# Attention over the paged cache: the first item's keys turned earlier, page loads held back, a new order of the steps around the window riders

## The chip, the cores and the metric

One core of one Trainium2 chip runs the whole program. The metric is the device time of one execution in microseconds, the median of several. Below, PE is TensorE (PEld its weight loads), DVE is VectorE, ACT is ScalarE, POOL is GpSimd and SP is SyncE, which here only issues transfers.

## The reference, cut to what matters

One decoder layer is computed for a prompt of 2048 positions and for 8 samples of 8 new positions each. The change lies where the samples' latent attention (`mla_sample`) begins: every sample attends to 8192 past positions that lie in pages of a cache, with 8 heads that share one latent key of width 256 and one rotary key of width 32.

```python
ckv_past = cache_ckv[l, page_table].reshape(Bd, past, KV_LORA)
kr_past = cache_krope[l, page_table].reshape(Bd, past, QK_ROPE)
...
s_past = jnp.einsum('bthc,bkc->bhtk', q_lat, ckv_past) + jnp.einsum('bthr,bkr->bhtk', q_rope, krope_past)
...
p, _ = masked_softmax_stats(jnp.concatenate([s_past, s_new], axis=-1) * MLA_SCALE, mask)
...
return (jnp.einsum('bhtk,bkc->bthc', p[..., :P], ckv_past)
        + jnp.einsum('bhtk,bkc->bthc', p[..., P:], ckv_new))
```

Beside it each sample has a dilated window attention over its last 2048 keys (`dilated_sample`, three patterns) and a cross-attention into 256 memory tokens. All these outputs are gated, projected and added to the residual.

## The kernel before, in words

The program is a chain of stages, each a block in which every engine runs its own list of instructions: input projection, the prompt's windows, latent projections, `prompt_latent_attention`, then a block with `sample_attention` and the output projection. Engines wait for each other only by semaphores, and within an engine the order is that of the code. A barrier (L3077) stands between the blocks.

**The prompt's attention** works on 32 units (`NU`), each two heads by 256 queries. An order `STEPS` made once and walked by all engines mixes scores, turns of probabilities (`turn`), values and the turning back of outputs (`back`). DVE copies half of every turned block (`keep_turned`, L1867) and does the last division (`finish`, L1877). The last two units are short (two and one pair of key blocks). POOL ends this stage with indirect loads (L1693 to L1699) of the first three pages of the cache (`EARLY` = 3), each of 1024 positions, and of their rotary keys.

**The samples' attention** takes the pages two by two: an item n is the pages 2n and 2n+1 of one sample, and there are 32 items (`NPAIR`), four to a sample. Item by item:

- DVE turns the keys (`turn_keys(l, k)`, L2455 for the two halves of a page, L2457 for the rotary keys); a page's pieces raise `k_turned` by 3. Before the loop it turns pages 0 and 1; in the loop it turns the pages of item n+1 while PE works on item n, except that for n = 0 the maximum of item 0 comes first.
- PE computes the scores in two parts, `score(n, 0, 4)` and `score(n, 4, CB + 1)`. By the trace's count the first is 64 matmuls and the second 80, the last 16 of them rotary (all L2179). Between and behind them stand parts of the values of the item before, `value(n - 1, lo, hi)` (L2214), positions 0 to 2 (12 matmuls) and 3 to 7 (20 matmuls). The end of positions 3 and 7 raises `pv_done`.
- DVE takes the maximum (`maxima`, L2463, L2464), ACT the exponentials (L2382), PE turns the probabilities (`turn_probs`, L2201, 16 matmuls), ACT copies them (L2375), DVE adds up (`accumulate`).

**Riders.** The window and memory attention of the 8 samples ride on items: `RIDES` = {3: 0, 6: 1, 9: 2, 13: 3, 16: 4, 19: 5, 23: 6, 26: 7}. At the end of such an item PE turns the window's keys (`turn_rows`, L2230), does the item's values, and scores the first 1024 keys (`score_rows(s, 0)`, L2256). The next item, the rider item (`rider_before(n)` gives its sample s), does the rest: window probabilities of both parts are turned (`turn_rows_probs`, L2268, L2270) and copied by ACT (`keep_rows_probs`, L2395), the second part is scored (`score_rows(s, 1)`, L2243 to L2246), and both parts' values are made (`value_rows`, L2286 and L2278 to L2280). DVE takes their maxima (`maxima_of_rows`, L2471) and copies the results (L2493).

**Loads.** POOL loads pages by `load_page(l)`: an indirect load of rotary keys (L2113) and one of the latent rows (L2118), 8 slots ahead (`AHEAD`). Pages 3 to 9 are issued without a wait; the later ones wait for `k_turned` and for `pv_done` of the page that was in the slot. SP loads the window of sample s (`load_window`, nine issues for keys, nine for values, and the memory's), the first one when `pv_done` reaches 3.

Of the kernel before, what the change touches and what calls it, by code (L numbers as in the profile page):

```python
# [17 lines left out]
P = 128  # L18
# [512 lines left out]
class Host:  # L531
# [7 lines left out]
    def __init__(self, b, zero, ident):  # L539
# [3 lines left out]
        self.pages_loaded, self.pages_kr_loaded = ([b.sem(f"{n}_loaded{l}") for l in range(self.EARLY)] for n in ("page", "page_kr"))  # L543
        self.k_raw = self.buf[:, 0:SEQ]
# [869 lines left out]
def prompt_latent_attention(nc, io, prompt, sample, host, owner):  # L1414
# [98 lines left out]
    with ExitStack() as stack:  # L1513
# [7 lines left out]
        pages_ahead = b.sb("pages_ahead", [P, Host.EARLY - 1, SEQ])  # L1521
        q_parts = b.sb("q_parts", [P, QBUF, 4, CW], F32R)
# [317 lines left out]
        def vector(dve):  # L1840
# [39 lines left out]

            dve.wait_ge(masks, 1)

            for what, a, p in STEPS:
# [6 lines left out]
                elif what == "turn":  # L1890
                    keep_turned(a, p)
                elif what == "back":
                    finish(a)

        return FirstUnit(load_first, load_third, cast_first, cast_third, split_first, split_third), pages_ahead, Programs(sync, gpsimd, tensor, scalar, vector)


# [26 lines left out]
def sample_attention(nc, io, sample, late, host, pages_ahead, stack, memory, owner):  # L1924


    GK = 8 * PAGE
# [100 lines left out]
    def sync(sp, output):  # L2028
# [74 lines left out]
    def gpsimd(pool):  # L2103
# [20 lines left out]
        pool.wait_ge(k_turned, 3 * EARLY)  # L2124
# [28 lines left out]

    def lanes_of(k, c, r):
# [6 lines left out]
    def tensor(pe, output):  # L2161
        def score(n, lo, hi):
# [3 lines left out]
            for k in range(lo, hi):  # L2166
                for h in range(2):
                    for g in range(4):
                        lanes = slice(UNIT * g, UNIT * g + UNIT)
                        out = scores[h * Q:(h + 1) * Q, g, 0:2 * P]  # L2170
                        if k < CB:
                            lhs = q_quad[lanes, s % 2, k, :]
                            rhs = turned[n % 2][lanes, :, h * HALF:(h + 1) * HALF, k * UNIT:(k + 1) * UNIT]
                            out = out.rearrange("q (i m t) -> q i m t", i=2, t=UNIT)
                        else:
                            lhs = q_rot[lanes, s, :]
                            rhs = krT[lanes, n % 2, :, h * P:(h + 1) * P]
# [5 lines left out]
        def wait_for_keys(n, s):  # L2183
# [7 lines left out]
            pe.wait_ge(k_turned, 6 * n + 6)  # L2191
# [114 lines left out]
        for n in range(NPAIR):  # L2306
# [23 lines left out]
            if s is not None:  # L2330
                value_rows(n, s, 1)
# [31 lines left out]
    def scalar(act, output):  # L2363
# [39 lines left out]
        for n in range(NPAIR):  # L2403
            s = rider_before(n)
            if s is not None:
                exponentials_of_rows(s, 0)
                keep_rows_probs(s, 0)
                exponentials_of_rows(s, 1)
            if n == LEFT + 1:
# [6 lines left out]
            if s is not None:  # L2416
# [816 lines left out]
```

## Time and profile before

| | |
|---|---|
| median of 3 runs | 1922.42 us (1918.53 to 1926.72) |
| the profiled execution | 1921.31 us, its span 1919.7 us |
| PE busy | 1795.3 us, 94% of the span |
| DVE, ACT, POOL busy | 1081.9, 810.2, 416.0 us |
| first score of item 0 starts | 1071.7 us from the span's start |
| exponentials of item 0, of item 31 start | 1092.5 us, 1515.9 us |

The span is what the profiler saw of one execution. Times of single instructions below are microseconds from the span's start. Matmuls overlap, so that PE's busy share says little about its pace; the idle time before an instruction and what ended it say more.

### The profile page before, as it was taken

The numbers are of one execution on the slowest core, as the hardware profiler recorded it, in microseconds if no ns is written. First come the engines' busy times: TensorE is split into PE (matmuls) and PEld (weight loads), VectorE is DVE, ScalarE is ACT, GpSimd is POOL, SyncE is SP. The second block draws the span as 40 slices with busy tenths as digits, with TensorE's granted clock in tenths as the row PEclk, the third lists the DMA queues.
The fourth block names the chain that finished last, engine by engine and source line by source line (L and its number), as shares of the span: only waits on it lengthen the run. The fifth ranks groups of instructions, "written<-read, shape, count | busy, mean of one in ns | idle before, by whom it ended". The sixth has DMA issues, their size and how long they took to land. (4 is left out here: it accounts for less than half of the span.)

```text
span 1919.7 us, 46575 instructions
## 1 busy us (share of the span) xinstructions
PE 1795.3 (94%) x18256; PEld 1370.1 (71%) x18256; DVE 1081.9 (56%) x2808; ACT 810.2 (42%) x1778; POOL 416.0 (22%) x567
## 2 busy tenths in 40 slices
PE   7999999999999899999999588988888889999998
PEld 6988988767787666776776355555555678888886
DVE  5443433787745677677766465666656853333343
ACT  5332322887723455565555132222222543333332
POOL 0101101274021230232012322232322311211110
PEclk9999999999999999999999699999999999999999
DMA  8746554733476410121102587888985574444441
GB/s 297 178 101 138 118 114 109 238 114 121 126 197 198 147 41 18 48 75 33 27 18 97 197 226 224 247 247 248 249 244 203 173 197 124 139 126 126 145 135 65
DMA packets 301372, 281.58 MB, mean 147 GB/s; under 512 B 146008, under 2 KB 262568, under 8 KB 292264
## 3 DMA queue, kind: packets, MB, share of 16 engines
q1 hardware_dynamic: 282840, 186.60, 38.1%
q0 software_dynamic: 18352, 92.44, 13.0%
q8 instruction: 130, 2.13, 0.5%
q14 instruction: 50, 0.41, 0.1%
HBM read 215.09 MB, written 55.48 MB: 141 GB/s over the span
## 5 line engine op out<-in xcount | busy, mean ns | idle before, releaser
L104 PE MATMUL proj_acc<-proj_w_hi,proj_x_hi 128*128 128x512 f32 (+2 forms) x512 | 182.4, 356 | 10.8 <-DVE proj_x_lo L362 8.7
L105 PE MATMUL proj_acc<-proj_w_lo,proj_x_hi 128*128 128x512 f32 (+2 forms) x512 | 181.9, 355 | 0.0
L106 PE MATMUL proj_acc<-proj_w_hi,proj_x_lo 128*128 128x512 f32 (+2 forms) x512 | 181.7, 355 | 0.0
L1851 DVE CUSTOM_DVE_ANT_0 mla_probs<-mla_scores,keep_in_rms 128x512 f32<-128x512 f32 x192 | 124.8, 688 | 59.4 <-PE mla_scores L1725 59.1
L1801 ACT ACTIVATE mla_probs<-mla_probs,mla_bias 128x256 f32<-128x256 f32 (+15 forms) x128 | 153.1, 1197 | 8.1 <-DVE mla_bias L1855 7.0
L1725 PE MATMUL mla_scores<-prompt_kr_parts,mla_q_parts 64*128 64x512 f32 (+3 forms) x640 | 135.3, 367 | 0.0
L2382 ACT ACTIVATE dec_probs<-dec_scores,sample_nb 128x1024 f32<-128x1024 f32 x32 | 35.7, 1114 | 207.5 <-DVE sample_nb L2464 176.9
L104 PEld LDWEIGHTS proj_acc<-proj_w_hi,proj_x_hi 128*128 128x128 f32 x512 | 97.4, 190 | 22.2 <-issue 8.7
L105 PEld LDWEIGHTS proj_acc<-proj_w_lo,proj_x_hi 128*128 128x128 f32 x512 | 97.5, 190 | 10.6
L106 PEld LDWEIGHTS proj_acc<-proj_w_hi,proj_x_lo 128*128 128x128 f32 x512 | 97.3, 190 | 10.4
L2179 PE MATMUL dec_scores<-late_turned,sample_q_lat 32*64 32x256 f32 x2048 | 85.2, 398 | 20.8 <-issue 12.0
L883 ACT ACTIVATE win_probs<-win_probs,win_rec 128x256 f32<-128x256 f32 (+1 forms) x192 | 86.8, 456 | 18.4 <-DVE win_rec L919 18.1
L1750 PEld LDWEIGHTS mla_turned<-host_ident,mla_probs 64*128 64x128 f32 x2180 | 80.5, 140 | 15.7 <-ACT mla_probs L1801 8.7
L1725 PE MATMUL mla_scores<-mla_even_k_hi,mla_q_parts 64*128 64x512 f32 (+3 forms) x320 | 80.2, 407 | 9.6 <-DVE mla_lowest L1851 7.8
L1750 PE MATMUL mla_turned<-host_ident,mla_probs 64*128 64x64 f32 x2180 | 84.7, 224 | 4.6 <-ACT mla_probs L1801 4.5
L106 PE MATMUL fin_gate<-fin_wg_hi,fin_x_lo 128*128 128x512 f32 x224 | 87.2, 389 | 0.0
L104 PE MATMUL fin_gate<-fin_wg_hi,fin_x_hi 128*128 128x512 f32 x224 | 87.2, 389 | 0.0
L105 PE MATMUL fin_gate<-fin_wg_lo,fin_x_hi 128*128 128x512 f32 x224 | 87.1, 389 | 0.0
L2179 PEld LDWEIGHTS dec_scores<-late_turned,sample_q_lat 32*64 32x64 f32 x2048 | 50.9, 135 | 49.0 <-issue 42.6
L2179 PE MATMUL dec_scores<-dec_keysT,sample_q_lat 32*64 32x256 f32 x2048 | 77.6, 394 | 7.4 <-issue 4.0
L1851 DVE CUSTOM_DVE_ANT_0 mla_probs<-mla_scores,mla_mask 128x256 f32<-128x256 f32 (+3 forms) x128 | 57.7, 488 | 46.5 <-PE mla_scores L1725 45.8
L1664 POOL CAST mla_q_parts<-host_buf 128x256 fp32r<-128x256 f32 x31 | 12.8, 414 | 314.3 <-DMA host_buf<-mla_qr 162.8
(462 smaller groups left out, 4490.3 us busy)
## 6 DMA issues: line engine op xcount, KB each, us to landing
featT<-proj_blocks SPq DMA_DIRECT2D x68, 180.0 KB, 4.9
win_v_tile<-wv_out SPq DMA_DIRECT2D x75, 128.0 KB
memory_x_raw<-in_xT SPq DMA_DIRECT2D x17, 512.0 KB, 5.4
proj_rows<-in_x SPq DMA_DIRECT2D x17, 512.0 KB, 3.8
late_ckv<-in_xT SPq DMA_DIRECT2D x17, 512.0 KB, 6.7
late_ckv<-in_x SPq DMA_DIRECT2D x17, 512.0 KB, 3.9
y_out<-host_buf POOLq DMA_DIRECT2D x16, 512.0 KB, 6.5
late_ckv<-late_ckv SPq DMA_DIRECT2D x248, 32.0 KB, 1.8
```

Of the source, the lines that this page charges most:

```text
L104: pe.matmul(out, lh, rh, start=start, stop=False)
L105: pe.matmul(out, lh, rl, start=False, stop=False)
L106: return pe.matmul(out, ll, rh, start=False, stop=stop)
L883: act.activation(pr, pr, ACT.Exp, bias=low[:, h:h + 1], scale=-1.0, accum_out=total[:, h:h + 1]).then_inc(exp_done, 1)
L1664: pool.tensor_copy(qn_hi[:, v, :], qn_raw[:, u % 2, :]).then_inc(q_high, 1)
L1725: mm = pe.matmul(scores[:, at % 3, 0:n], lhs[rows, :], rhs[rows, :], start=a == 0, stop=a == len(parts) - 1)
L1750: mm = pe.transpose(turned[:, r % 2, lane, (kb * 2 * QB + w) * 64:(kb * 2 * QB + w + 1) * 64], probs[rows, u % 2, w, src * P:(src + 1) * P ...
L1801: act.activation(row, row, ACT.Exp, bias=bias[:, at:at + 1], scale=-1.0, accum_out=total[:, at:at + 1]).then_inc(exp_done, 1)
L1851: dve.tensor_tensor_reduce(probs[:, u % 2, w, c * CH:c * CH + wide], scores[:, n % 3, 0:wide], add, -MLA_SCALE, -LOWEST, ALU.add, ALU.min, ...
L2179: mm = pe.matmul(out, lhs, rhs, start=k == 0, stop=k == CB)
L2382: act.activation(probs[:].rearrange("p j (r k) -> p r j k", r=4), scores[:, :, 0:2 * P].rearrange("p r (j k) -> p r j k", k=UNIT), ACT.Exp ...
```

## The change

There are three parts.

1. The keys of item 0 (pages 0 and 1) are turned by DVE at the end of the prompt's attention, in six pieces, two behind each of the three last copies of turned blocks (`turn_first_keys`). They go to a part of the prompt's `probs` buffer that the last unit doesn't use, and have a semaphore of their own, `first_keys`. `k_turned` so counts 6 fewer everywhere.
2. In the samples' block, `load_page(6)` and all that is behind it on POOL wait for the scores of item 0, and so do SP's first four loads.
3. Order. In rider items PE scores the second part of the window first, then turns the first part's probabilities, does three quarters of the remaining latent scores, turns the second part's probabilities, ends the scores and does both value groups ahead of `turn_probs`; ACT copies the second part's probabilities ahead of the item's exponentials; DVE takes the second maximum ahead of the second page's first half. In the other items, values 0 and 1 instead of 0 to 2 stand between the two parts of the scores and values 2 to 7 behind.

```diff
@@ prompt_latent_attention
+        first_keys = probs[:, 1, :, :].rearrange("p (i h) t -> p i h t", i=2)
+        KEYS_AT, KR_AT = SEQ // 2, SEQ // 2 - host.KR
...
+            def turn_first_keys(k):
+                l, half = divmod(k, 2)
+                if k == 0:
+                    dve.wait_ge(ring_done, last_turn(NU - 5) + 1)
+                    dve.wait_ge(ring_done, last_turn(NU - 3) + 1)
+                if k < 4:
+                    src = pages_ahead[:, 0, :] if l else host.page
+                    dve.wait_ge(host.pages_loaded[l], 16)
+                    dve.transpose(first_keys[:, l, half, KEYS_AT:], src[:, half * KEYS_AT:(half + 1) * KEYS_AT]).then_inc(host.first_keys, 1)
+                else:
+                    dve.wait_ge(host.pages_kr_loaded[half], 16)
+                    dve.transpose(first_keys[:, half, 0, KR_AT:KEYS_AT], host.pages_kr[half]).then_inc(host.first_keys, 1)
...
                 elif what == "turn":
                     keep_turned(a, p)
+                    if a >= NU - 2 and pieces < 6:
+                        for k in range(pieces, pieces + 2):
+                            turn_first_keys(k)
+                        pieces += 2
@@ sample_attention, sync
+        sp.wait_ge(scores_done, 1)
         for dst, f in ((qbT, FB_QB), (kbT, FB_KB), (qcT, FB_QC)):
@@ gpsimd
             if l >= AHEAD + EARLY:
-                pool.wait_ge(k_turned, 3 * (l - AHEAD) + 3)
+                pool.wait_ge(k_turned, 3 * (l - AHEAD) - 3)
+            if l == AHEAD - 2:
+                pool.wait_ge(scores_done, 1)
...
-        pool.wait_ge(k_turned, 3 * EARLY)
+        pool.wait_ge(k_turned, 3 * EARLY - 6)
@@ tensor
+    def keys_at(n, h):
+        if n == 0:
+            return first_keys[:, :, h, SEQ // 2:].rearrange("p i (m c) -> p i m c", c=KVL)
+        return turned[n % 2][:, :, h * HALF:(h + 1) * HALF, :]
...
-            pe.wait_ge(k_turned, 6 * n + 6)
+            if n:
+                pe.wait_ge(k_turned, 6 * n)
+            else:
+                pe.wait_ge(host.first_keys, 6)
...
             if s is not None:
+                score_rows(s, 1)
                 turn_rows_probs(n, s, 0)
-                score_rows(s, 1)
+                score(n, 4, 7)
+                turn_rows_probs(n, s, 1)
+                score(n, 7, CB + 1)
+                value_rows(n, s, 0)
+                value_rows(n, s, 1)
             elif n:
-                value(n - 1, 0, 3)
-            score(n, 4, CB + 1)
-            if s is not None:
-                value_rows(n, s, 0)
-                turn_rows_probs(n, s, 1)
-            elif n:
-                value(n - 1, 3, M)
+                value(n - 1, 0, 2)
+                score(n, 4, CB + 1)
+            else:
+                score(n, 4, CB + 1)
+            if s is None and n:
+                value(n - 1, 2, M)
...
             turn_probs(n)
-            if s is not None:
-                value_rows(n, s, 1)
@@ scalar
                 exponentials_of_rows(s, 1)
+                keep_rows_probs(s, 1)
...
             exponentials(n)
-            if s is not None:
-                keep_rows_probs(s, 1)
@@ vector
-        for l in range(2):
-            for k in range(3):
-                turn_keys(l, k)
...
-                turn_keys(2 * n + 3, 0)
                 if s is not None:
                     maxima_of_rows(s, 1)
+                turn_keys(2 * n + 3, 0)
```

## Rows read from the trace of the kernel before

**Rows 1.** Windows around the start of the sample attention, all engines

```profile
1066.00:1072.00 6.00, 0.32 (x8) 0.35 (x16) 5.28 (x6) 0.00 (x0) 3.98 (x5) 0.50 0.59 165
...
1072.00:1091.00 19.00, 14.33 (x144) 7.40 (x131) 0.02 (x1) 0.00 (x0) 10.85 (x12) 0.59 0.98 394
...
1091.00:1098.00 7.00, 1.33 (x24) 1.18 (x32) 6.96 (x9) 2.41 (x4) 2.02 (x3) 0.50 0.07 18
```

**Rows 2.** Timeline, item 0: start us, us, engine, line, what, idle before

```profile
1066.26 2.37 DVE L2455 STREAM_TRANSPOSE late_turned<-host_buf 128x1024 f32<-128x1024 f32 x2 [2.43 <-PEq L3077]
...
1066.81 0.96 POOL L2113 DMA_INDIRECT dec_kr<-in_cache_kr,sample_rows_of  x1 [23.28 <-POOLq L3077]
...
1071.65 2.45 PEld L2179 LDWEIGHTS dec_scores<-late_turned,sample_q_lat 32*64 32x64 f32 x50 [8.58 <-issue]
...
1077.88 0.21 PEld L2179 LDWEIGHTS dec_scores<-late_turned,sample_q_lat 32*64 32x64 f32 x4 [1.22 <-issue]
...
1083.19 0.95 POOL L2118 DMA_INDIRECT late_ckv<-in_cache_ckv,sample_rows_of  x1 [0.30 <-issue]
...
1086.39 2.44 PEld L2179 LDWEIGHTS dec_scores<-late_turned,sample_q_lat 32*64 32x64 f32 x50 [1.23 <-issue]
...
1090.98 1.23 DVE L2463 TENSOR_REDUCE dec_gmax<-dec_scores 128x1 f32<-128x1024 f32 x1 [19.45 <-PE dec_scores L2179]
...
1097.79 3.72 PE L2179 MATMUL dec_scores<-dec_keysT,sample_q_lat 32*64 32x256 f32 x64 [2.92 <-DVE dec_krT L2457]
```

**Rows 3.** Timeline, last unit of the prompt's attention, DVE

```profile
1056.07 0.68 DVE L1867 COPY prompt_q_nope<-mla_turned 128x512 f32<-128x512 f32 x1
...
1058.67 0.69 DVE L1867 COPY prompt_q_nope<-mla_turned 128x512 f32<-128x512 f32 x1 [1.92 <-PE mla_turned L1750]
...
1063.40 0.42 DVE L1877 TENSOR_TENSOR mla_out<-mla_turned,mla_inv 128x256 f32<-128x256 f32 x1 [1.21 <-issue]
```

**Rows 4.** Timeline, a plain item, its POOL issues and the next item's first

```profile
1208.77 0.95 POOL L2118 DMA_INDIRECT dec_more<-in_cache_ckv,sample_rows_of  x1 [18.36 <-PE dec_outs L2214]
...
1212.54 0.96 POOL L2113 DMA_INDIRECT dec_kr<-in_cache_kr,sample_rows_of  x1 [0.30 <-issue]
...
1214.41 0.72 PEld L2179 LDWEIGHTS dec_scores<-dec_keysT,sample_q_lat 32*64 32x64 f32 x28 [1.19 <-issue]
...
1215.52 1.52 PE L2214 MATMUL dec_outs<-dec_more,dec_pT 128*64 128x256 f32 x12
...
1219.48 1.23 DVE L2463 TENSOR_REDUCE dec_gmax<-dec_scores 128x1 f32<-128x1024 f32 x1 [3.43 <-PE dec_scores L2179]
...
1220.24 0.95 POOL L2118 DMA_INDIRECT dec_more<-in_cache_ckv,sample_rows_of  x1 [6.74 <-PE dec_outs L2214]
...
1222.25 0.71 PE L2201 MATMUL dec_p_turned<-host_ident,dec_probs 64*128 64x64 f32 x16 [0.57 <-ACT dec_probs L2382]
```

**Rows 5.** Timeline, an item with a rider

```profile
1185.67 0.95 POOL L2118 DMA_INDIRECT late_ckv<-in_cache_ckv,sample_rows_of  x1 [2.66 <-PE dec_outs L2214]
...
1191.33 0.74 PEld L2179 LDWEIGHTS dec_scores<-dec_keysT,sample_q_lat 32*64 32x64 f32 x28 [0.96 <-issue]
...
1194.49 0.40 DVE L2471 CUSTOM_DVE_ANT_0 dec_probs_win<-dec_side,dec_ways_mask 128x264 f32<-128x264 f32 x1
...
1196.38 1.95 PE L2286 MATMUL dec_outs<-dec_v_rows,dec_pT_win 128*64 128x256 f32 x16
...
1200.09 0.71 PE L2201 MATMUL dec_p_turned<-host_ident,dec_probs 64*128 64x64 f32 x16 [1.43 <-ACT dec_pT_win L2395]
...
1201.75 0.47 PE L2179 MATMUL dec_scores<-late_turned,sample_q_lat 32*64 32x256 f32 x7
```

**Rows 6.** Timeline, the first rider's values

```profile
1152.38 2.49 PE L2286 MATMUL dec_outs<-dec_v_rows,dec_pT_win 128*64 128x256 f32 x16 [3.57 <-DMA dec_mem_v<-in_mem_v]
```

**Rows 7.** Waits of PE, 1160 to 1500 us: total, times, longest

```profile
PE dec_p_turned L2201 <- ACT dec_pT_win L2395: 10.3, 7, 1.7
```

**Rows 8.** One window of the steady part, columns as in rows 1

```profile
1200.00:1242.00 42.00, 37.47 (x678) 23.31 (x680) 25.56 (x42) 11.28 (x22) 11.45 (x12) 1.00 0.88 254
```

More of the change, by code:

```diff
@@ L543, in __init__ @@
         self.pages_loaded, self.pages_kr_loaded = ([b.sem(f"{n}_loaded{l}") for l in range(self.EARLY)] for n in ("page", "page_kr"))
+        self.first_keys = b.sem("first_keys")
         self.k_raw = self.buf[:, 0:SEQ]
@@ L1879, in finish @@
                                   inv[:, rows].rearrange("p (w o) -> p w o", o=1).broadcast_to([P, 2 * QB, VH]), ALU.mult).then_inc(turned_dve, 1)
+            def turn_first_keys(k):
[10 more added lines that the diff above has]
+                    dve.transpose(first_keys[:, half, 0, KR_AT:KEYS_AT], host.pages_kr[half]).then_inc(host.first_keys, 1)
             dve.wait_ge(masks, 1)
+            pieces = 0
             for what, a, p in STEPS:
@@ L1891, in vector @@
                     keep_turned(a, p)
+                    if a >= NU - 2 and pieces < 6:
+                        for k in range(pieces, pieces + 2):
+                            turn_first_keys(k)
+                        pieces += 2
                 elif what == "back":
                     finish(a)
-        return FirstUnit(load_first, load_third, cast_first, cast_third, split_first, split_third), pages_ahead, Programs(sync, gpsimd, tensor, scalar, vector)
+        return FirstUnit(load_first, load_third, cast_first, cast_third, split_first, split_third), (pages_ahead, first_keys), Programs(sync, gpsimd, tensor, scalar, vector)
 class LateWeights:
@@ L1921, in __init__, with sample_attention @@
         self.x_high, self.x_low, self.gained, self.w_high, self.mix_stored = (b.sem(n) for n in ("x_high", "x_low", "gained", "w_high", "mix_stored"))
-def sample_attention(nc, io, sample, late, host, pages_ahead, stack, memory, owner):
+def sample_attention(nc, io, sample, late, host, ahead, stack, memory, owner):
+    pages_ahead, first_keys = ahead
     GK = 8 * PAGE
@@ L2152, in gpsimd, with rotary_at @@
             pool.dma_start(mix[:, :, MIX_A + h * HD:MIX_A + (h + 1) * HD], acc_win[rows, 0, :, cols]).then_inc(win_stored, 16)
+    def keys_at(n, h):
+        if n == 0:
+            return first_keys[:, :, h, SEQ // 2:].rearrange("p i (m c) -> p i m c", c=KVL)
+        return turned[n % 2][:, :, h * HALF:(h + 1) * HALF, :]
+    def rotary_at(n, h):
+        if n == 0:
+            return first_keys[:, :, 0, SEQ // 2 - host.KR + h * P:SEQ // 2 - host.KR + (h + 1) * P]
+        return krT[:, n % 2, :, h * P:(h + 1) * P]
     def lanes_of(k, c, r):
@@ L2172, in score @@
                             lhs = q_quad[lanes, s % 2, k, :]
-                            rhs = turned[n % 2][lanes, :, h * HALF:(h + 1) * HALF, k * UNIT:(k + 1) * UNIT]
+                            rhs = keys_at(n, h)[lanes, :, :, k * UNIT:(k + 1) * UNIT]
                             out = out.rearrange("q (i m t) -> q i m t", i=2, t=UNIT)
@@ L2176, in score @@
                             lhs = q_rot[lanes, s, :]
-                            rhs = krT[lanes, n % 2, :, h * P:(h + 1) * P]
+                            rhs = rotary_at(n, h)[lanes, :, :]
                             out = out.rearrange("q (i t) -> q i t", i=2)
@@ L3075, in program @@
             nc.clear_and_free_semaphores(projecting.sems)
-            first, pages_ahead, attention = prompt_latent_attention(nc, io, prompt, sample, host, keep)
+            first, ahead_pages, attention = prompt_latent_attention(nc, io, prompt, sample, host, keep)
             with nc.Block() as block:
@@ L3108, in program @@
         memory = stack.enter_context(ExitStack())
-        samples, attention = sample_attention(nc, io, sample, late, host, pages_ahead, stack, memory, keep)
+        samples, attention = sample_attention(nc, io, sample, late, host, ahead_pages, stack, memory, keep)
         memory.close()
```

## The prediction

> **What bounds the kernel now.** I read the granted busy times by window first, then the timeline of the stretches that the diff touches, then the waits of PE. In the windows around the start of the sample attention the columns are: stretch, its length, busy time and count of PE, PEld, DVE, ACT, POOL, then the granted clock as a share of 2.4 GHz, the DMA share and GB/s. The reader is to see three things there [rows 1]: six microseconds in which DVE turns keys and PE has all but nothing to do, nineteen in which one item's scores (144 matmuls) fill the whole window with DMA at 0.98, and seven in which PE waits again for DVE, all near the 1.2 GHz level.
>
> The timeline says why [rows 2]. PE's first scores start at 1071.65, when six transposes begun at 1066.26 are done. PE loads 50 weights at full pace and then only four at a time, about every 1.4 us, and is back at full pace at 1086.39. POOL issues indirect page loads from 1066.81 without a pause; the last of sixteen starts at 1083.19. The scores take 1071.65 to 1090.98, 19.3 us, and item 1's start at 1097.79, 6.8 us later, since DVE turns its keys only after item 0's maximum.
>
> The same slow-down stands in every item in small. In a plain item [rows 4] POOL's four issues begin at 1208.77 (1.26 us apart) and PE's full pace returns at 1214.41, which is 5.64 after the first issue. In a rider item [rows 5] it is 1185.67 and 1191.33, 5.66. Of the groups of four issues with PE in the first scores there are 17, between 1138 and 1465 us, and all of them read 5.64 to 5.69; these two stand for them. So the plain items run in a loop: the values at position 3 release POOL, 5.65 us later PE regains its pace, does what is left of the first scores, the values, the second scores and again the values at position 3. POOL to POOL is 1220.24 - 1208.77 = 11.47. The 0.57 us in which PE stands idle before it turns the probabilities [rows 4] is not what sets that period, and this decides what the new order is worth.
>
> **The keys of item 0.** Six transposes, 5.3 us of DVE (1066.26 to 1071.6), leave the start of the sample attention and go to the end of the prompt's. There two of the large ones (2.37) come ahead of the copy at 1056.07, two ahead of the copy at 1058.67, which DVE awaited for 1.92, and the two small ones (0.8) ahead of the last divisions [rows 3]. Hidden are the 1.92 and the 1.21 waited before 1063.40; PE turns and adds up other blocks meanwhile. The late copies hold the back transposes by 0.7 us and the last division comes behind the small transposes: I take the prompt's end 1.2 us later (bounds 0, and 5.5 - 1.9 = 3.6). The next block starts at 1067.5 and PE with it, 4.1 us before 1071.65.
>
> **The page loads.** Pages 3, 4 and 5 are six issues from about 1068.0 to 1068.0 + 5 x 1.26 + 0.95 = 1075.3; pages 6 to 9 wait. SP's four small loads wait too; they are read in item 1 and land long before. PE's full pace came back 0.9 us [rows 4] to 2.3 us [rows 2] after the end of the last issue, so at 1076.2 to 1077.6 instead of 1086.39. By then PE has run some 55 matmuls and a dozen at the slow pace; the rest is what took 1086.39 to 1090.98, 4.6 us. Item 0's scores end at about 1081, 10 us earlier.
>
> That is not kept. Item 1 starts 6.8 us later, at about 1087.8, again 10 us earlier, but now eight page issues run beside it (1081.3 to 1091), then POOL's memsets and the first half of page 10, to about 1095. Before, POOL was nearly idle there (2.02 us of work in seven [rows 1]). PE has its stock of some 50 weight loads less 16 transposes, then the slow pace. I take 4 us lost (below: 2, when the stock lasts; above: 8, when it crawls until 1096 at 1.2 GHz). Item 1's scores then end 6 us earlier (bounds 2 and 8).
>
> The Trainium skill ("Runtime: NRT & Kernel Launch", instruction fetch mechanics) says that an engine fetches its instructions in 16 KiB blocks over a queue of its own and that the cost is mostly hidden. No row here shows the cause of the slow pace; by that rule page loads need not cause it, item 0 would keep its 19.3 us and the sum below would hold 4.1 instead of 6.
>
> **The first rider.** SP starts the first window's loads at the third value of item 1's first page, so they start 6 us earlier and land 6 us earlier; the rider waited 3.57 us for them and began its values at 1152.38 [rows 6]. From there the new order leaves out the turn and copy between its two value groups: 1.3 us.
>
> **The other seven riders.** Now [rows 5] the scores end at 1196.38, the window's first values take 1.9, then PE waits 1.43 for ACT's copy of the window's second probabilities, seven times and 10.3 us in all [rows 7]; the turn of 0.64 follows and 1.02 of values until 1201.75. After the change that copy is made before the item's exponentials. The price: the second row scores come first, the window's maximum (DVE, 1194.49) waits for them and for a turn, until about 1194.1 to 1194.8, and DVE's three transposes (2.8 us) follow it instead of one preceding it. Scores end at about 1197.0 (a wait of 0.35 and the small turn of 0.24 lie before), the item's maximum starts at 1197.5 instead of 1196.56. PE has both value groups to do, until 1199.9. From maximum to turn takes 1222.25 - 1219.48 = 2.77 [rows 4], so the turn starts at 1200.3 and the next item at 1200.9: 0.85 us earlier; where DVE starts with its transposes sooner, 1.05. I take 0.9 (bounds 0.4, a DVE yet later, and 1.43). No page issue lies between 1191.33 and the next item, so it is kept: 7 x 0.9 = 6.3 us.
>
> **The plain items.** Four matmuls of the values go behind the scores (1.52 us for twelve [rows 4], so about 0.43). Scores and maximum are 0.43 earlier, the turn too, within the idle 0.57. But POOL is released at position 3 of the values: four matmuls earlier by the scores, four later by the values, so at the same time, and PE regains its pace at that plus 5.65. PE only meets the slow stretch sooner. I price it at 0 for 10 items, half (0.24) for the 7 in which a window is turned, where PE next waits for ACT and not for pace (1.7 us), and 0.5 for item 29, behind which no page is loaded. Bounds: 0, and 0.43 for all 18 items, 7.7.
>
> Changed semaphore counts with the same meaning cost nothing. Behind the stage everything is released by its items, so the shift goes through to the end.
>
> **Sum:** 6 + 1.3 + 6.3 + 1.7 + 0.5 = 15.8 us. The profiled execution took 1921.3 (its span 1919.7), 1.1 below the median of 1922.4: 1905.5 for it, 1906.5 for a median.
>
> **Rivals.**
> 1. *Plain items keep their gain.* The pace returns with the instructions, not with POOL's clock. For it: the 0.57 idle is real. Against: the constant 5.65. 21.3 us, 1901.
> 2. *Item 1 gives all of it back.* POOL's eight issues, memsets and page 10 hold PE as sixteen held item 0. For it: POOL is busy from 1081 to 1095 in both views. Against: only half as long. 9.8 us, 1912.6.
> 3. *The slow pace is not POOL's.* Item 0 still takes 19.3 us, the start alone gains 4.1: 13.9 us, 1908.5.
> 4. *Slower: the transfers bound the stage.* The seventh issue moves from 1074.4 to 1081.3. If the DMA queues were full throughout, these 7 us would come out at the end and the riders' gain with them be lost: 1929. It decides from a share of 1.0 on; the steady window has 0.88 [rows 8], and DVE never waited for a page. The first window's loads are where it would begin: PE waited for them already [rows 6].
> 5. The diff does what it says in any case: the semaphores order it.
>
> **How the numbers follow.** Chances: forecast 0.47, rival 1 0.17, rival 2 0.18, rival 3 0.10, rival 4 0.08. A measurement tells apart about 0.5%, 9.6 us, so faster means below 1912.8. The forecast by itself spans 1901 to 1912 by its bounds, with little beyond. Faster: nearly all of the forecast, rivals 1 and 3, and half of rival 2, 0.78; the same 0.17; slower 0.05. The range takes rivals 1, 2 and 3 with their bounds: 1895 to 1918.
>
> **What would show it.** In the changed kernel: the first scores near 1067.5 without transposes between block start and them; item 0's scores at most 14 us long with PE's full pace back 1 to 2.3 us after POOL's sixth issue; item 1's scores longer than before's 8 us, beside POOL's eight issues; POOL to POOL in plain items still 11.4 to 11.5, with PE's idle before the turn gone and a longer slow stretch; rider items 0.9 shorter with the 1.43 wait gone and the maximum following DVE's last transpose at once. I am wrong if plain items run 11.0, if item 1 is as quick as before, or if the first window's values start less than 4 us earlier.

## The result, and the profile after

| | before | after |
|---|---|---|
| median | 1926.49 us (1918.53 to 1927.49, 5 runs) | 1906.46 us (1904.76 to 1912.33, 5 runs) |
| ratio after to before | | 0.9911, 95% interval 0.9882 to 0.9941 |
| the profiled execution, its span | 1921.31, 1919.7 us | 1905.70, 1904.0 us |

By the ratio the kernel became faster by 17 us, 0.9% (the medians lie 20.0 us apart, the means 16.9). On another chip, later, the two medians were 1929.32 and 1914.78, ratio 0.9921 (0.9901 to 0.9941). The forecast was 1906.5, or 15.8 us less. The size is right. That the forecast median meets the measured one to a tenth is luck: it was counted from 1922.42, and before's median of five runs is 1926.49. The sections below show that one step inside its largest term had the wrong sign and that three smaller terms had little ground, and that the errors cancelled. Below, a gain in us that stands beside a ratio is worked out from the ratio.

First the start of the stage. The windows of the changed kernel cover the stretch before item 0's scores, the scores, and the stretch up to item 1's scores (columns as in [rows 1]).

```profile
1070.00:1072.40 2.40, 0.00 (x0) 0.02 (x1) 0.00 (x0) 0.00 (x0) 0.00 (x0) 0.50 0.19 55
1072.40:1085.10 12.70, 10.80 (x144) 6.47 (x144) 0.00 (x0) 0.00 (x0) 5.70 (x6) 0.63 0.74 277
1085.10:1091.90 6.80, 1.12 (x16) 0.93 (x17) 6.74 (x9) 2.41 (x4) 5.01 (x6) 0.50 0.71 219
```

The 144 matmuls now take 12.7 us; in [rows 1] they filled 19. The timeline of the changed kernel shows the pieces of it, and below them a rider item and a plain item.

```profile
1060.06 2.36 DVE L1892 STREAM_TRANSPOSE mla_probs<-host_buf 128x1024 f32<-128x1024 f32 x2
...
1062.91 2.35 DVE L1892 STREAM_TRANSPOSE mla_probs<-mla_pages_ahead 128x1024 f32<-128x1024 f32 x2
...
1072.38 2.90 PEld L2214 LDWEIGHTS dec_scores<-mla_probs,sample_q_lat 32*64 32x64 f32 x59 [4.50 <-issue]
...
1072.89 0.95 POOL L2138 DMA_INDIRECT dec_kr<-in_cache_kr,sample_rows_of  x1 [25.40 <-POOLq L3113]
...
1078.49 0.20 PEld L2214 LDWEIGHTS dec_scores<-mla_probs,sample_q_lat 32*64 32x64 f32 x5 [1.21 <-issue]
...
1079.17 0.95 POOL L2143 DMA_INDIRECT late_ckv<-in_cache_ckv,sample_rows_of  x1 [0.30 <-issue]
...
1079.91 0.31 PEld L2214 LDWEIGHTS dec_scores<-mla_probs,sample_q_lat 32*64 32x64 f32 x4 [1.21 <-issue]
...
1081.35 1.63 PEld L2214 LDWEIGHTS dec_scores<-mla_probs,sample_q_lat 32*64 32x64 f32 x37 [0.54 <-issue]
...
1085.36 0.95 POOL L2138 DMA_INDIRECT dec_kr<-in_cache_kr,sample_rows_of  x1 [5.25 <-PE dec_scores L2214]
...
1188.65 0.60 ACT L2435 ACTIVATE dec_pT_win<-dec_p_turned 128x512 f32<-128x512 f32 x1 [0.48 <-PE dec_p_turned L2308]
...
1189.59 1.49 PEld L2324 LDWEIGHTS dec_outs<-dec_v_rows,dec_pT_win 128*64 128x64 f32 x16 [0.38 <-ACT dec_pT_win L2435]
...
1192.90 0.57 PEld L2239 LDWEIGHTS dec_p_turned<-host_ident,dec_probs 64*128 64x128 f32 x16 [0.39 <-ACT dec_probs L2422]
...
1241.40 0.95 POOL L2143 DMA_INDIRECT late_ckv<-in_cache_ckv,sample_rows_of  x1 [17.13 <-PE dec_outs L2252]
...
1247.04 0.73 PEld L2214 LDWEIGHTS dec_scores<-late_turned,sample_q_lat 32*64 32x64 f32 x29 [1.19 <-issue]
...
1252.89 0.95 POOL L2143 DMA_INDIRECT dec_more<-in_cache_ckv,sample_rows_of  x1 [6.76 <-PE dec_outs L2252]
...
1254.46 0.58 PEld L2239 LDWEIGHTS dec_p_turned<-host_ident,dec_probs 64*128 64x128 f32 x16 [0.59 <-ACT dec_probs L2422]
```

Four readings, against [rows 2 to 5]. PE loads 59 weights at full pace, then four to six at a time, mostly every 1.4 us, and is back 1.23 us after POOL's sixth issue has ended (1080.12). Before, POOL made fourteen issues in a row (pages 3 to 9, two each, 1066.81 to 1083.19 at 1.26 us); the sixteen of the prediction is a miscount. In the plain item PE is back at 1247.04, 5.64 after POOL's first issue, and POOL to POOL is 1252.89 - 1241.40 = 11.49: [rows 4] gave 5.64 and 11.47. In the rider item ACT's second copy lies ahead of the values, and the weight loads of the turn, at 1192.90, come 0.39 after those of the last value: the wait of 1.43 in [rows 5] is gone. The transposes of item 0's keys stand in the prompt, DVE's copies behind them are late, and the stage begins later for it.

Since the stages ahead differ by several us from one execution to the next (the last `k_nope` copy of the prompt starts at 1055.47 before, at 1059.45 after, and no line of the change lies ahead of it), distances within the stage say more than times. The table counts from that copy to the exponentials of item 0, and from there on between exponentials, all read from timelines of one execution each. "Clock falls" are the items 6 to 31 in which the granted clock is under 1.00.

| kernel | copy to 0 | 0 to 1 | 1 to 3 | 3 to 5 | 5 to 31 | 31 to end | clock falls |
|---|---|---|---|---|---|---|---|
| before | 37.02 | 14.89 | 20.39 | 39.76 | 348.33 | 403.84 | 0 |
| after | 27.19 | 19.21 | 20.26 | 34.02 | 340.19 | 403.68 | 0 |
| after, again | 27.22 | 18.68 | 20.69 | 34.42 | 352.07 | 407.25 | 4 |
| keys and gate | 27.96 | 16.29 | 20.67 | 40.14 | 351.24 | 402.11 | 0 |
| gate alone | 23.63 | 19.34 | 20.56 | 34.36 | 348.88 | 404.21 | 0 |
| riders' order alone | 36.20 | 15.52 | 20.83 | 35.57 | 340.71 | 405.98 | 0 |
| plain order alone | 36.56 | 14.96 | 20.55 | 34.65 | 355.65 | 406.67 | 3 |
| after, old plain order | 27.58 | 19.47 | 20.93 | 34.22 | 349.48 | 406.70 | 3 |
| after, without keys | 25.89 | 17.85 | 20.59 | 35.90 | 360.46 | 404.16 | 9 |
| the same, pages spread | 26.27 | 14.89 | 27.20 | 36.18 | 352.68 | 404.31 | 5 |
| gate and riders' order | 25.60 | 18.23 | 21.00 | 35.44 | 348.71 | 404.70 | 2 |
| the same, values halved | 23.91 | 21.54 | 22.19 | 32.57 | 361.02 | 403.30 | 1 |
| fewer issues | 27.08 | 18.98 | 19.45 | 33.46 | 307.79 | 405.73 | 0 |
| plain issues | 21.46 | 14.88 | 22.16 | 37.81 | 304.03 | 401.98 | 0 |

### The profile page after: what moved, and what is told of

Its sections match the earlier page's. It is cut to its first block and busy times, and to the rows that moved or that the text cites. A ratio compares the mean times of both kernels' runs of the same rounds, so it can differ in the third digit from the quotient of the medians.

```text
span 1904.0 us, 46574 instructions
## 1 busy us (share of the span) xinstructions
PE 1801.5 (95%) x18256; PEld 1372.4 (72%) x18256; DVE 1079.4 (57%) x2808; ACT 809.8 (43%) x1778; POOL 414.9 (22%) x567
## 3 DMA queue, kind: packets, MB, share of 16 engines
q0 software_dynamic: 18352, 92.44, 13.1%
## 5 line engine op out<-in xcount | busy, mean ns | idle before, releaser
L884 ACT ACTIVATE win_probs<-win_probs,win_rec 128x256 f32<-128x256 f32 (+1 forms) x192 | 86.6, 453 | 23.3 <-DVE win_rec L920 22.9
L2214 PE MATMUL dec_scores<-late_turned,sample_q_lat 32*64 32x256 f32 x1920 | 73.5, 384 | 7.7 <-issue 7.2
L1816 ACT ACTIVATE prompt_q_nope<-mla_turned 128x512 f32<-128x512 f32 x72 | 42.5, 593 | 86.4 <-PE mla_turned L1753 84.5
```

The source lines that it names most:

```text
L884: act.activation(pr, pr, ACT.Exp, bias=low[:, h:h + 1], scale=-1.0, accum_out=total[:, h:h + 1]).then_inc(exp_done, 1)
L1816: act.activation(dst, src, ACT.Copy).then_inc(turned_act, 1)
L2214: mm = pe.matmul(out, lhs, rhs, start=k == 0, stop=k == CB)
```

## The experiments

Twelve kernels in three groups; each group shares one chip and its runs of the kernel before. "Page gate" is part 2 of the change.

### One part at a time

**Keys and gate.** The changed kernel with both old orders.

```diff
             if s is not None:
-                score_rows(s, 1)
                 turn_rows_probs(n, s, 0)
-                score(n, 4, 7)
-                turn_rows_probs(n, s, 1)
...
+                score_rows(s, 1)
+            elif n:
+                value(n - 1, 0, 3)
+            score(n, 4, CB + 1)
```

> The changed kernel with the riders' and the plain items' old order: the first item's keys are turned at the prompt's end and pages from the sixth on wait, no more. Mine, from the two traces: the first items alone are worth about 10 us, since by the changed kernel's trace the exponentials of item 5 came 11.4 us earlier counted from the last copy of the prompt's turns, and about 1.3 of that is the first rider's order. Time about 1916, ratio to before 0.995. Rival, the prediction's own size: the start is worth 6 us and no more, 1920, ratio 0.997; then the exponentials of item 5 come about 6 us earlier, and the first window's values still wait for their loads. In both: item 0's scores 12 to 14 us instead of 19.3, item 1's longer than 8.

Measured: 1915.8 us, ratio 0.9956 (0.9942 to 0.9971), 8.5 us faster (7.6 by medians), between the two. By the trace item 5's exponentials are 7.0 us earlier from the copy on, nearer to the rival's 6, and the first window's values still waited for their load:

```profile
1148.19 2.38 PE L2324 MATMUL dec_outs<-dec_v_rows,dec_pT_win 128*64 128x256 f32 x15 [3.54 <-DMA dec_mem_v<-in_mem_v]
```

**The riders' order alone.** The kernel before with that part of the diff in `tensor`, `scalar` and `vector`.

> The kernel before with the riders' new order alone. Mine: the seven later riders and the items behind them gain about 8.5 us between the exponentials of item 5 and item 31 (as between the two traces), the first rider 1.3 or less, together 9 to 10: about 1916.5, ratio 0.995; the first window's values still wait for their loads near 1152. Rival A: the order also took away the first window's wait, 5.7 instead of 1.3, together 14: 1912, ratio 0.9925. Rival B: riders are worth the 6.3 of the prediction and what more there was came from the plain order: 1919, 0.9965.

Measured: 1910.82, ratio 0.994 (0.9917 to 0.9962). Items 5 to 31 take 7.6 us less than before, as in the changed kernel's trace (8.1) and in no kernel with the old riders; the other kernels with the new ones have falls of the clock in this stretch. The wait for the values' load is there (2.87 us), so rival A's reason falls, though its 1912 us fits the time; rival B's 0.9965 lies just outside the interval. In this trace no fall of the clock follows the wait, and items 3 to 5 take 4.2 us less than in the trace of before, where one did. The 4.2 and the 7.6 come to 11.8, near the 11.5 us of the ratio, but both are read from one execution each.

**The plain order alone.** The kernel before with `value(n - 1, 0, 2)` and `value(n - 1, 2, M)`.

> The kernel before with the plain items' new split of the values alone (positions 0 and 1 before the second part of the scores, 2 to 7 behind). Mine: nothing, within 1 us of before, ratio 1.000; from POOL's first issue to the next item's 11.47 as before, the idle time of PE before the turn gone and the slow stretch longer. Rival (the prediction's first): each plain item keeps 0.43 us, POOL to POOL 11.04, 7.7 us in all, ratio 0.996. Second rival: the seven items in which a window is turned keep 0.24 each, 1.7 us.

Measured: 1924.95, ratio 1.0009 (0.9991 to 1.0028): nothing, as the loop through POOL says; the interval leaves out the 7.7 us of the first rival and reaches just to the second's 1.7.

**The gate alone.** The kernel before with two waits.

```diff
+        sp.wait_ge(scores_done, 1)
         for dst, f in ((qbT, FB_QB), (kbT, FB_KB), (qcT, FB_QC)):
...
+            if l == AHEAD - 2:
+                pool.wait_ge(scores_done, 1)
```

> The kernel before, with pages from the seventh load on (and SP's four small loads) waiting for the first item's scores, and nothing else: keys turned at the start of the stage as before. Mine (PE's slow pace goes with POOL's issues): POOL makes six issues instead of sixteen beside item 0, PE's full pace is back about 1 to 2.3 us after the sixth has ended, some 8 us earlier than before, and item 0's scores take about 11 to 12 us instead of 19.3; item 1's, beside eight issues, take longer than before and give back about 4, so 3 to 4 us stay at the exponentials of item 1, ratio about 0.998. Rival (the slow pace is not POOL's): item 0's scores keep 19.3 us, nothing gained, ratio 1.000. Second rival: item 1 gives all back: item 0's exponentials 7 us earlier, item 1's none.

Measured: 1912.96, ratio 0.9945 (0.9923 to 0.9966): no slower than with the keys moved as well, and well below the 0.998 expected. Its timeline:

```profile
1073.05 0.95 POOL L2116 DMA_INDIRECT dec_kr<-in_cache_kr,sample_rows_of  x1 [23.34 <-POOLq L3080]
...
1077.89 5.01 PEld L2182 LDWEIGHTS dec_scores<-late_turned,sample_q_lat 32*64 32x64 f32 x128 [8.57 <-issue]
...
1079.32 0.95 POOL L2121 DMA_INDIRECT late_ckv<-in_cache_ckv,sample_rows_of  x1 [0.30 <-issue]
...
1084.08 0.95 POOL L2116 DMA_INDIRECT dec_kr<-in_cache_kr,sample_rows_of  x1 [3.81 <-PE dec_scores L2182]
```

All 128 latent scores run without a break and item 0's scores take 6.2 us, where 11 to 12 were expected. PE starts 4.8 us after POOL, behind DVE's transposes, and POOL's sixth issue is over (1080.27) 2.4 us after PE's start, about when PE has made the 50 to 59 loads that it gets through at full pace in the traces of before and after. The four other kernels with the gate and without the keys' move show the same unbroken 128. The six transposes that the change takes away from here were the cover of POOL's issuing. Which part of the gain is owed to POOL's wait and which to SP's was not tried apart.

### Is it POOL's issuing, or the bytes?

Two kernels on the changed one; in the second the rotary keys' load is changed in the same way. The first leaves out most loads of rotary keys, the second the page table, so neither makes the full result; they only tell about time.

```diff
 # fewer issues
-    loads_of = lambda l: 32 * (l // AHEAD + (1 if l % AHEAD >= EARLY else 0))
+    loads_of = lambda l: 16 * (l // AHEAD + (1 if l % AHEAD >= EARLY else 0)) + 16
...
-            pool.indirect_dma_start(kr[:, u, :], None, kr_rows, rows).then_inc(page_loaded[u], 16)
+            if l < AHEAD + EARLY:
+                pool.indirect_dma_start(kr[:, u, :], None, kr_rows, rows).then_inc(page_loaded[u], 16)
 # plain issues
-            pool.indirect_dma_start(slots[u].rearrange("p m c -> p (m c)"), None, ckv_rows, rows)
+            pool.dma_start(slots[u].rearrange("p m c -> p (m c)"), ckv_rows[l * P:(l + 1) * P, :])
```

> The changed kernel with the rotary keys loaded for the first eleven pages only; afterwards the scores use what lies there (the output's rotary part is therefore wrong). This halves POOL's issues and leaves 8/9 of the bytes (1024 of 1152 KB a page). If the slow pace goes with the issues: a group is two issues instead of four, and PE's full pace is back about 3 to 3.9 us after the first one starts, instead of 5.65; plain items run about 1.8 to 2.6 us shorter, near 9 to 9.7 us (or where DVE or ACT then ends last), and the kernel gains 30 us or more. Rival: it goes with the bytes in flight: back after 5.0 to 5.65 us, plain items 11 us or more, 8 us gained at most. Second rival: something else fixes the period of 11.47, which then stays.

> The changed kernel with every page load made by a plain DMA from POOL's queue of as many bytes, from fixed rows of the cache instead of the rows in the page table (so the output is of other pages): the same bytes at the same places, without indirection. If the slow pace comes of POOL working out the indirect rows: the issues on POOL are far shorter than 0.95 us or PE keeps its full pace beside them, plain items fall under 10 us. Rival: it comes of the bytes: the stretch keeps its 5 to 5.65 us and plain items 11.3 or more. If POOL's issues of plain loads last as long as the indirect ones and the stretch stays, the run tells nothing between them.

Measured: 1871.11, ratio 0.9698 (0.9667 to 0.9729) with half the issues, and 1860.99, ratio 0.9641 (0.961 to 0.9671) with plain ones. The plain kernel's page has the same transfers in POOL's queue as the changed kernel's, byte for byte and packet for packet:

```profile
q0 software_dynamic: 18352, 92.44, 13.4%
```

(changed kernel: 18352, 92.44, 13.1%). Its timeline at an item, and the window of [rows 8]:

```profile
1343.20 0.54 POOL L2143 DMA_DIRECT2D dec_more<-in_cache_ckv  x1 [18.04 <-PE dec_outs L2252]
...
1345.40 1.53 PEld L2214 LDWEIGHTS dec_scores<-late_turned,sample_q_lat 32*64 32x64 f32 x64
...
1345.47 0.55 POOL L2138 DMA_DIRECT2D dec_kr<-in_cache_kr  x1
...
1352.07 0.54 POOL L2143 DMA_DIRECT2D host_buf<-in_cache_ckv  x1 [6.05 <-PE dec_outs L2252]
```

```profile
1200.00:1242.00 42.00, 41.33 (x820) 26.33 (x817) 31.02 (x51) 13.70 (x26) 8.65 (x16) 1.00 1.00 300
```

The 64 loads of the first scores run through beside POOL's issues, POOL to POOL is 8.87 us instead of 11.47, and this at a DMA share of 1.00 and 300 GB/s where [rows 8] had 0.88 and 254. So neither the bytes nor full queues slow PE; the indirect issues do. The same kernel shows it at item 0, with the keys moved and POOL's six issues from 1070.46 on:

```profile
1070.17 6.03 PEld L2214 LDWEIGHTS dec_scores<-mla_probs,sample_q_lat 32*64 32x64 f32 x128 [4.49 <-issue]
```

Item 0's scores run without a break here too, and its exponentials come 21.46 us after the copy, where the changed kernel needs 27.19 and the gate alone 23.63: with plain issues the keys' earlier start is kept.

Two issues do less harm than four: with the rotary keys left out PE's break in the item of 1359 us is

```profile
1359.58 0.94 POOL L2144 DMA_INDIRECT host_buf<-in_cache_ckv,sample_rows_of  x1 [7.93 <-PE dec_outs L2253]
1361.31 0.94 POOL L2144 DMA_INDIRECT late_ckv<-in_cache_ckv,sample_rows_of  x1 [0.78 <-PE dec_outs L2253]
...
1362.61 0.64 PEld L2215 LDWEIGHTS dec_scores<-dec_keysT,sample_q_lat 32*64 32x64 f32 x20 [0.27 <-issue]
```

0.27 us, PE is back 3.03 us after the first issue, and plain items take 9.3 to 11.1.

### Without the keys' move

**The changed kernel without it.** Keys turned at the start of the stage, counts as before; everything else as changed.

> The changed kernel with the first item's keys turned at the start of the stage again (as before): the gate on the pages and both new orders stay. Mine: moving the keys costs. With the gate alone item 0's scores started 5.5 us later, but POOL's six issues lay beside the transposes, PE met no slow stretch, and item 0's exponentials came 3.6 us earlier (counted from the last copy of the prompt's turns) than in the changed kernel. So this kernel is 3 to 4 us faster than the changed one: ratio to before about 0.989, time 1902 to 1904; item 0's scores one run of 144 matmuls in some 6 us. Rival (the prediction's): the keys are worth 3 to 4 us, this kernel is slower than the changed one, 1910, ratio 0.993.

Measured: 1914.02, ratio 0.9915 (0.989 to 0.9939), the same as the changed kernel's 0.9911 and 0.9921; the 0.989 expected and the rival's 0.993 both lie within the interval. A part was missed at the start. Item 0's exponentials came 1.3 us earlier than in the changed kernel, of 3 to 4 expected, since the stage itself began 1.4 later in this execution (POOL's first issue 12.8 us after the copy, 11.3 with the gate alone, by the same instructions). The rest was lost between items 5 and 31, where nine items run with a fallen clock. The windows behind one slow stretch, from 1246.30:

```profile
1246.30:1248.30 2.00, 1.64 (x33) 1.26 (x32) 1.93 (x3) 0.00 (x0) 0.00 (x0) 0.61 0.96 325
1248.30:1250.30 2.00, 2.00 (x19) 0.77 (x8) 0.00 (x0) 0.00 (x0) 0.00 (x0) 0.53 1.09 395
```

PE had loaded four weights in the 1.4 us before 1246.66, and then ran at the 1.2 GHz level for some 3.4 us (granted clock 0.53 to 0.61 in these windows); the item took 13.19 us instead of 11.5. The changed kernel's own first trace has no such item.

**Pages spread.** The same, with pages 8 and 9 behind the memsets and held until item 1's scores.

```diff
-        for l in range(EARLY, AHEAD + 2):
+        for l in range(EARLY, AHEAD):
             load_page(l)
...
+        pool.wait_ge(scores_done, 2)
-        for l in range(AHEAD + 2, NP):
+        for l in range(AHEAD, NP):
             load_page(l)
```

> The kernel without the keys' move and with pages 8 and 9 (four more issues, and page 10's first) held back until the second item's scores; POOL's memsets and the window's constants come before them. If PE's pace goes with POOL's issues and PE has a stock of some 36 weight loads, four issues (5 us) beginning with item 0's maximum are over before item 1's scores start 6.5 us later: item 1's scores meet no slow stretch, 2 to 4 us earlier at the exponentials of item 1, of which item 2, with four issues more beside it, gives back about 1.3. Ratio about 0.988, 1 to 2.5 us below the kernel without this. Rival: the slow stretch is only put off, items 2 and 3 give all back: the same time as without it. Second rival: later pages are missed by DVE in item 4 or 5 and it is slower.

Measured: 1918.22, ratio 0.9945 (0.9922 to 0.9969), so no gain: the means differ by 4.0 us, plus or minus 6.0, to its disadvantage. The first half of my theory held: item 1 meets no slow stretch (14.89 us instead of 17.85). The second half did not: item 2 takes 16.86, because its scores start at once and lie beside POOL's issues whole. In the kernel without the spread item 1 waits some 6.5 us for its keys, and five of its eight issues lie under that wait. From item 0's exponentials to item 3's the spread takes 42.09 us, 3.7 more than without it, so the rival holds and more: all is given back.

```profile
1089.71 2.92 PEld L2183 LDWEIGHTS dec_scores<-dec_keysT,sample_q_lat 32*64 32x64 f32 x64 [3.08 <-issue]
...
1103.78 0.21 PEld L2183 LDWEIGHTS dec_scores<-late_turned,sample_q_lat 32*64 32x64 f32 x4 [1.24 <-issue]
...
1108.14 1.22 PEld L2183 LDWEIGHTS dec_scores<-late_turned,sample_q_lat 32*64 32x64 f32 x27 [1.13 <-issue]
```

### The parts that gain, alone

**Gate and riders' order.** The kernel before with these two, keys and plain items as before.

> The kernel before with the gate and the riders' new order; the first item's keys and the plain items' split as before. If the gate (0.9945 alone) and the riders' order (0.994 alone) add up and the other two parts only cost: ratio 0.9885, some 5 us below the changed kernel, plain items 11.5 us in all positions with the clock at 1.00. Rival: the plain items' slow stretch trips the clock here too in some of them (13.2 us, as in the kernel with the new split and no keys' move), and the ratio stays at 0.991.

Measured: 1907.91, ratio 0.9888 (0.9868 to 0.9909), with the changed kernel at 0.9921 on the same chip: the difference of the means of six runs each is 6.5 us, plus or minus 4.1. By the ratio it is the fastest of the kernels that load all their pages by the page table. Two plain items fell to the lower clock, so the old split does not exclude that.

**Values halved.** The same with `value(n - 1, 0, HALF)` and `value(n - 1, HALF, M)`.

> The same with the values split in halves: positions 0 to 3 before the second part of the scores, so that POOL may load over the item's first page some 3 us earlier; the second page's issues come when they came before. Two of the four issues then lie beside the second scores, two beside the turn, and the runs with half the issues showed a slow stretch of 0.3 to 1.1 us beside two of them. Mine: plain items 9.5 to 10.5 us instead of 11.5, 15 us or more gained over the kernel with three positions, ratio 0.975 to 0.981. Rival: four issues cost PE as much wherever they lie: plain items 11.2 or more, the same time within 4 us.

Measured: 1919.70, ratio 0.9949 (0.9929 to 0.9969): 11 us slower than with three positions, the wrong sign.

```profile
1388.46 0.95 POOL L2121 DMA_INDIRECT host_buf<-in_cache_ckv,sample_rows_of  x1 [3.86 <-PE dec_outs L2217]
...
1389.74 0.22 PEld L2182 LDWEIGHTS dec_scores<-late_turned,sample_q_lat 32*64 32x64 f32 x5 [0.54 <-issue]
1390.50 0.22 PEld L2182 LDWEIGHTS dec_scores<-late_turned,sample_q_lat 32*64 32x64 f32 x6 [0.54 <-issue]
...
1394.50 0.95 POOL L2121 DMA_INDIRECT late_ckv<-in_cache_ckv,sample_rows_of  x1 [3.84 <-PE dec_outs L2217]
...
1395.14 0.58 PEld L2204 LDWEIGHTS dec_p_turned<-host_ident,dec_probs 64*128 64x128 f32 x16 [1.38 <-ACT dec_probs L2387]
```

Two issues now break the second scores (three breaks of 0.5 us), which the maximum awaits, and only 16 matmuls of values are left to cover maximum and exponentials, so PE stands 1.38 us before the turn. Plain items take 12.2 us, and the loop is no longer POOL's.

**The changed kernel with the old plain order, and as it is.**

> The changed kernel with the plain items' old split (positions 0 to 2 before the second part of the scores). The prediction gives the new split 2.2 us (seven window items 0.24 each, 0.5 for item 29): 1 to 3 us slower than the changed kernel. Rival: the new split is worth nothing or costs, as in the kernel before (ratio 1.0009 alone, some window items 1 to 2 us longer): the same as the changed kernel or 2 to 5 us faster, item behind a rider 9.4 instead of 8.95, window items shorter by as much.

> The changed kernel as it is, beside the other three on the same chip. Ratio 0.991. Its trace shows whether items of 13.2 us at a lower clock, which the kernel without the keys' move had in its plain items, come in the changed kernel too from run to run, and whether the first rider waits for the window's values this time (3 us and a clock fall behind it) or not.

Measured: 1912.03, ratio 0.9909 (0.9889 to 0.993), and 1914.78, ratio 0.9921 (0.9901 to 0.9941). The new split is worth nothing here either: the means differ by 2.8 us, plus or minus 3.9, in favour of the old one. The second trace of the changed kernel has four items with a fallen clock (13.50, 13.56, 22.55 and 22.57 us, where the first had 11.91, 11.55, 20.35 and 20.36) and is 11.9 us longer between items 5 and 31. In the first of them PE's breaks are 1.24 and 1.23 us, the clock 0.66 behind them:

```profile
1204.44 0.19 PEld L2214 LDWEIGHTS dec_scores<-dec_keysT,sample_q_lat 32*64 32x64 f32 x3 [1.24 <-issue]
1205.86 1.07 PEld L2214 LDWEIGHTS dec_scores<-dec_keysT,sample_q_lat 32*64 32x64 f32 x35 [1.23 <-issue]
```

```profile
1206.50:1208.50 2.00, 2.00 (x33) 1.03 (x18) 0.94 (x2) 0.43 (x1) 0.00 (x0) 0.66 1.06 388
```

## Why the prediction was right, point by point

**The slow pace is POOL's** (rivals 3 and 4). Right. The direct loads with the same bytes show it. They also answer rival 4: the stage runs faster at a share of 1.00, and the only wait of PE or DVE for a page in that trace between 1160 and 1450 us is one of 0.2 us. The prediction's sixteen issues beside item 0 were fourteen; its sums rest on the times of the issues, which are right, and stay. The rule on instruction fetch of the Trainium skill ("Runtime: NRT & Kernel Launch", instruction fetch mechanics), that its cost is mostly hidden, decided nothing: no run here shows how an indirect issue holds PE back. The DMA view of before between 1071 and 1089 us has packets of POOL's queue alone and none of the two instruction queues, and the next one comes behind 1089.9, when PE has been back at full pace since 1086.39. So no block of instructions landed that could have ended this stretch.

**The keys of item 0 and the page loads** (6 us, of which 4.1 by an earlier start). The size holds, 5.5 us at item 1's exponentials; the attribution fails. The step that failed is the one that added the earlier start to the shorter scores. The gate alone brings 13.4 us at item 0 and 8.9 at item 1. With the keys moved the scores start 3.25 us earlier, but level with POOL's first issue, and they run into the slow stretch; with plain issues they don't, and the start is kept. POOL's first issue comes 13.2 to 14.3 us after the copy in the six traces with the keys moved and 11.3 to 13.0 in the eight without. Five traces with keys, gate and indirect loads have 27.1 to 28.0 us from the copy to item 0's exponentials, five with the gate alone or without the keys 23.6 to 26.3. In time: 2.9 plus or minus 3.6 us (keys and gate against gate) and 3.7 plus or minus 3.7 (old plain order in both); neither is clear of noise alone, the two together are (3.3 plus or minus 2.4). The third pair, the changed kernel with and without the move, shows no difference (0.9911 and 0.9921 against 0.9915), with nine fallen clocks in the latter's trace. By the first two the move costs about 3 us. What item 1 gives back, priced at 4, is 4.3.

**The prompt's end**, 1.2 us later: from copy to last division 1.6 us more in the changed kernel's first trace, and 2.0 to 3.0 more in its second, with keys and gate, and with the old plain order. This term was too small.

**The first rider**, 1.3 us. Mis-sized twice. Where the load is not waited for, the order is worth 0.3 (gate alone 34.36, changed kernel 34.02). The trace of after gained 5.7, since its window values did not wait. That goes with no part of the change: a wait of 2.9 to 3.6 us stands in before, keys and gate, the riders' order, gate with riders' order, pages spread and plain issues, one of 0.8 with the values halved, and none in the two traces of after, gate alone, plain order alone, after with the old plain order, after without keys and fewer issues. Where PE waits, its values begin 23.3 to 24.9 us after SP's issue of the load; where it doesn't, 20.7 to 23.9. When that load lands varies; why stays open. The sign "less than 4 us earlier" is met by the plain times (1152.38 and 1149.23) and not by the distance from the copy (7.1 us earlier), which is the one that tells about the stage.

**The other seven riders**, 6.3 us, and the plain part 2.2. Items 5 to 31 gained 8.1 of the 8.5 forecast, but all of it by the riders (7.6 alone). In time the riders' order brings 11.5 us; the traces show the excess over 8 between items 3 and 5 alone, with the first rider. In the two traces with the old riders in which PE waited 3.5 us for values, the clock fell behind the wait and the item took 17.1; in the three with the new order and a wait of 2.9 to 3.0 it did not (12.0 to 12.4). With plain issues the order is the new one and the wait 3.3, and there the clock fell and the item took 13.8. So a shorter wait, and not the order itself, may be what spares the clock; that this is the excess is argued, not shown.

**The plain items.** Priced at nothing for ten of them: right, POOL to POOL 11.49. The 0.24 for the seven window items and 0.5 for item 29 were wrong. Alone the split measures 1.0009.

**The sum.** By the ratios: gate 10.6 faster, riders 11.5 faster, keys about 3 slower, plain split about 2 slower or nothing: 17, as measured, each term with some 4 us of noise. The prediction had 6 for keys and gate together, where 8.5 were measured, and 9.8 for the two orders, where it was 11.5 less 1.7. Rival 2 (item 1 gives all back) and rival 1 (plain items gain) fell.

Open: what decides in which items the clock falls. Kernels with the new plain split had 0, 4, 3, 9 and 5 such items in their traces, with the old one 0, 0, 0, 0, 3 and 2 (and the halved one 1; fewer and plain issues, with the new split, 0 and 0). That is a hint against the new split, no proof, and the chips are a rival to it: of the four kernels on the last chip, those with the old split had 3 and 2 falls too and the new one 4, and the nine and the five come from a chip on which no kernel with the old split was traced. Taking the gate away and keeping the keys wasn't tried: page 6 lands where item 0's turned keys lie.

## What to carry to other kernels

Before moving work off a critical start, ask what it covers: with the page gate in place six transposes hide POOL's first issues, and without them PE meets the slow stretch that it escapes otherwise. A gate of two waits, which holds back loads that nobody needs yet, was worth 10.6 us, nearly as much as the riders' new order (11.5). And take the trace of one execution for the mechanism, not for the sum: two traces of the same kernel differ by 12 us in one stage.

## What the runs showed of the hardware

- While POOL makes indirect page loads (0.95 us each, 1.26 apart) PE gets through some 35 to 60 weight loads and then mostly four or five per 1.4 us, and is back 0.9 to 2.3 us after the last issue has ended (0.91 in [rows 4], 2.25 in [rows 2]). Plain loads of the same bytes from the same queue take 0.54 us each and leave PE alone. In this kernel that is worth about 50 us, ratio 0.9641 against 0.9911.
- Behind two breaks of 1.2 us in a row the granted clock sometimes falls to its lower level for some 3.4 us and sometimes not: in the second trace of the changed kernel it fell behind the pair that ends at 1205.86 and not behind a like pair that ends at 1388.66. The same item (16) took 11.55 and 13.56 us in two executions of one kernel.
